# Another layout of SBUF for the weight ring, the tokens and small tensors of a two-block transformer kernel

## The reference, cut to what matters

```python
def swiglu(h, w_in, w_out):
    a, b = jnp.split(h @ w_in, 2, axis=-1)      # w_in: 1024 x 5632
    return (jax.nn.silu(a) * b) @ w_out         # w_out: 2816 x 1024

proj = h @ w_in          # each mixer: 1024 x 1048 to 1024 x 4104
out = mixed @ w_out      # each mixer: 1024 x 1024
kv = rmsnorm(s, kv_norm) @ kv_w                              # 1024 x 1536, shared KV of NSA
jax.nn.silu(flat @ cmp_w1) @ cmp_w2                          # its compress step, w2: 256 x 64
```

## Time and profile before

| what | value |
|---|---|
| median of three runs | 1311.67 us |
| lowest, highest run | 1310.64, 1311.71 us |
| span of the profiled execution (first to last instruction) | 1310.3 us |
| mean granted TensorE clock | 0.992 |
| TensorE matmul busy | 1270.2 us, 97% |
| TensorE weight loads busy (beside the matmuls) | 1077.6 us, 82% |
| VectorE, ScalarE, GpSimd busy | 873.9, 613.6, 24.2 us |
| bytes read from HBM | 216.04 MB, 166 GB/s over the span |

### The profile page before, as it was taken

How to read it: one execution, slowest core, us unless ns; L and a number is a source line. 1 busy time by engine, 2 the same in 40 slices (tenths; PEclk the granted TensorE clock), 3 DMA queues, 4 the chain that set the end, 5 groups by cost and what they waited for, 6 DMA issues and landing times.

```text
span 1310.3 us, 16491 instructions
## 1 busy us (share of the span) xinstructions
PE 1270.2 (97%) x6717; PEld 1077.6 (82%) x6717; DVE 873.9 (67%) x1312; ACT 613.6 (47%) x839; POOL 24.2 (2%) x37
## 2 busy tenths in 40 slices
PE   6999999989999999999999999999999999999997
PEld 5888888988788888878888886778888899988876
DVE  6655557885755556685657569856555567566896
ACT  6444346435434445444435357654444344544461
POOL 2000000100000000000000000000000000000000
PEclk9999999999999999999999989999999999999999
DMA  9655545443555556565665440065666686446401
GB/s 329 207 182 187 186 162 185 142 155 129 183 184 185 188 192 186 166 193 170 217 224 169 159 161 1 1 200 187 191 193 193 130 217 172 150 130 211 176 2 65
DMA packets 158812, 218.17 MB, mean 167 GB/s; under 512 B 8257, under 2 KB 110993, under 8 KB 158737
## 3 DMA queue, kind: packets, MB, share of 16 engines
q1 hardware_dynamic: 156880, 212.56, 51.2%
q0 software_dynamic: 1376, 3.71, 0.9%
q10 hardware_dynamic: 480, 0.85, 0.2%
HBM read 216.04 MB, written 1.05 MB: 166 GB/s over the span
## 4 chain that ended last, share of the span: by engine, by line
PE 82%; DVE 11%; issue 3%; ACT 2%; SPq 1%; DMA 1%; DVEq 0%
PE PS L686 23%; PE PS L689 23%; PE PS L687 23%; DVE wlo L2050 2%; PE PS L823 1%; PE PS L721 1%; PE PS L722 1%; ACT whi L1523 1%; PE PS L706 1%; PE PS L1300 1%; DVE arena L2639 1%; PE PS L728 1%; PE PS L1016 1%; SPq L591 1%; DVE XL L2090 1%
## 5 line engine op out<-in xcount | busy, mean ns | idle before, releaser
L2050 DVE TENSOR_TENSOR wlo<-raw,whi 128x2048 fp32r<-128x2048 f32 (+4 forms) x206 | 457.4, 2230 | 122.6 <-ACT whi L1523 121.8
L1523 ACT ACTIVATE whi<-raw 128x2048 fp32r<-128x2048 f32 (+4 forms) x206 | 381.4, 1863 | 63.4 <-DMA raw<-in_fox_w_in_dram 33.1
L686 PE MATMUL PS<-whi,XL 128*128 128x512 f32 (+3 forms) x992 | 385.8, 390 | 8.9 <-DVE scr L2152 3.8
L687 PE MATMUL PS<-wlo,XH 128*128 128x512 f32 (+3 forms) x992 | 379.8, 384 | 0.0
L689 PE MATMUL PS<-whi,XH 128*128 128x512 f32 (+3 forms) x992 | 265.0, 384 | 0.0
L686 PEld LDWEIGHTS PS<-whi,XL 128*128 128x128 f32 x992 | 187.3, 189 | 45.1 <-DVE scr L2152 4.9
L689 PEld LDWEIGHTS PS<-whi,XH 128*128 128x128 f32 x992 | 185.5, 190 | 35.5
L687 PEld LDWEIGHTS PS<-wlo,XH 128*128 128x128 f32 x992 | 187.4, 189 | 32.9
L1577 ACT ACTIVATE scr<-PS,rn 128x256 f32<-128x256 f32 x88 | 41.7, 474 | 225.2 <-PE PS L689 223.9
L686 PE MATMUL PS<-whi,GL 128*128 128x512 f32 x320 | 125.4, 392 | 0.0
L687 PE MATMUL PS<-wlo,GH 128*128 128x512 f32 x320 | 124.6, 389 | 0.0
(11 more groups left out here) (387 smaller groups left out, 1339.2 us busy)
## 6 DMA issues: line engine op xcount, KB each, us to landing
raw<-in_ffn_w_in_dram SPq DMA_DIRECT2D x174, 512.0 KB, 5.0
raw<-in_ffn_w_out_dram SPq DMA_DIRECT2D x88, 512.0 KB, 4.9
raw<-in_fox_w_in_dram SPq DMA_DIRECT2D x24, 512.0 KB, 7.9
raw<-in_a_w_in_dram SPq DMA_DIRECT2D x16, 512.0 KB, 4.6
raw<-in_dsa_w_in_dram SPq DMA_DIRECT2D x16, 512.0 KB, 6.0
raw<-in_kv_w_dram SPq DMA_DIRECT2D x12, 512.0 KB, 4.2
raw<-in_fox_w_in_dram SPq DMA_DIRECT2D x12, 344.0 KB, 5.0
raw<-in_a_w_out_dram SPq DMA_DIRECT2D x8, 512.0 KB, 4.9
```

The source lines that it names most:

```text
L686: mm(o, xl, wh, start=start and i == 0, stop=False, skip_group_check=True)
L687: mm(o, xh, wl, start=False, stop=False, skip_group_check=True)
L1523: A(whi[:, p % SLOTS, 0:n], raw[:, p % SLOTS, 0:n], ACT.Copy).then_inc(hi_done, 1)
L2050: V.tensor_tensor(wlo[:, p % SLOTS, 0:n], raw[:, p % SLOTS, 0:n], whi[:, p % SLOTS, 0:n].bitcast(F32), ALU.subtract).then_inc(lo_done, 1)
```

## The change

It changes addresses only.

- Each row of `whi`, `wlo` and `raw` is 2048 + 16 elements long (`SHIFT`), and the last 16 are not used, so slot s begins 64 s bytes further than it would without.
- `par`, `ss`, `rv`, `ry`, `rt`, `rr`, `nmin` and `zsum`, 1920 bytes of each partition in all, are allocated ahead of `whi` instead of behind `con`.
- `w2s`, the small weights of the compress step (1 KiB), becomes a part of `arena` (elements 12032 to 12288) instead of a tensor of its own.

The addresses that result, in bytes of a partition: `whi` 18432 (9 x 2048), `wlo` and `raw` 76224, `h` 134016, `XH` 142208, `XL` 150400, `xs` 158592, `GH` 166784, `GL` 168832, `arena` 178400. Slots of `whi` begin 64 s above a multiple of 2048, slots of `wlo` 448 + 64 s above one; the token tensors `XH`, `XL`, `GH` and `GL` begin 896 above one.

```diff
+SHIFT = 16
...
-        whi = sb("whi", [P, SLOTS, PIECE], F32R)
+        par = sb("par", [P, P])
+        ss = sb("ss", [P, 32])
+        rv = sb("rv", [P, 32])
+        ry = sb("ry", [P, 32])
+        rt = sb("rt", [P, 32])
+        rr = sb("rr", [P, 32])
+        nmin = sb("nmin", [P, 96])
+        zsum = sb("zsum", [P, 96])
+        whi = sb("whi", [P, SLOTS, PIECE + SHIFT], F32R)[:, :, 0:PIECE]
         lo_at = (nc.sbuf_base + 31) // 32 * 32
-        wlo = sb("wlo", [P, SLOTS, PIECE], F32R)
-        raw = nc.alloc_sbuf_tensor_at("raw", [P, SLOTS, PIECE], F32, offset=lo_at)
+        wlo = sb("wlo", [P, SLOTS, PIECE + SHIFT], F32R)[:, :, 0:PIECE]
+        raw = nc.alloc_sbuf_tensor_at("raw", [P, SLOTS, PIECE + SHIFT], F32, offset=lo_at)[:, :, 0:PIECE]
...
-        w2s = sb("w2s", [P, 2, 2, HD])
...
         rowsb = arena[:, 0:P]
+        w2s = arena[:, 12032:12288].rearrange("p (c k d) -> p c k d", c=2, k=2)
```

More of the change, by code:

```diff
@@ L170, in program @@
         con = sb("con", [P, C_ALL])
-        par = sb("par", [P, P])
         qgain = sb("qgain", [P, 1])
-        w2s = sb("w2s", [P, 2, 2, HD])
         bif = sb("bif", [HEADS, 3])
[L175 to L179, removed]
         lns = sb("lns", [P, 8])
@@ L184, in program @@
         r2 = sb("r2", [P, 2])
-        nmin = sb("nmin", [P, 96])
-        zsum = sb("zsum", [P, 96])
         rz = sb("rz", [P, 96])
```

## The result

The changed kernel takes 1324.84 us (median of four runs, 1322.35 to 1326.38) against 1311.66 us before; the ratio is 1.0098, with a 95% interval of 1.0081 to 1.0115. The forecast of no change was wrong. Its range, up to 1328 us, holds the time, which is that of the rival "steps of 512 columns no longer settle", 1324 us.

A forecast was written before the change was run, and what follows sets the result against it. The prediction took back-to-back weight matmuls on PE to bound the kernel, so addresses matter mainly through their spacing. Its terms summed to 0, giving 1311.5 us (no change, chance 0.37), with a range of 1297 to 1328 us.

The forecast's parts named there:

- steps of 512 columns no longer settle: Slower case for PE's weight matmuls: steps stay at their pace after a wait; 1324 us, chance 0.31.
- What bounds the kernel: Whole kernel: time is mostly the number of weight-product matmuls times the distance between them; PE holds 82% of the chain.
- terms of 0: VectorE's and ScalarE's splits (-1 to +1 us), ring loads (-0.7 to +0.7) and `w2s`: each taken as no change.
- The reading of the rows: Weight matmuls in the earlier trace: some 13 ns, 32 cycles, extra per step, taken as a cost of PE's two reads.
- PE's reading: Cost of changed operand distances within 512 bytes on PE's matmuls: taken as 0, low end -14.5 us.
- The bounds: Ends for PE's matmuls: -14.5 us, or +14 to +20 us if 3100 steps lose 4.6 to 6.6 ns, less 2.
- The slower rival: 512-column steps settle only at operand distance 0 within 512 bytes, which most slots lose; 1324 us, chance 0.31.
- sign of recognition: If distance within 512 bytes decides, pace differs by slot and products from slot 6 of `whi` stay at 226.7 ns.
- The faster rival: Weight matmuls: distance 0 makes operands collide most, so spreading slots helps; -14.5 us, 1297 us, or -3 to -8; chance 0.32.
- The rule of two independent ports: PE reads each operand through its own port, so weight loads cost no bandwidth; 512 columns every 215.7 ns, layout effect 0.
- A2: Theory added during the experiments: 512-column steps settle at 226.7 ns only with both operands at the same place within 256 bytes.

The follow-up runs named there:

- m1: Matmuls alone, model's work left out, other engines idle, 48 per segment at chosen operand distances; 512 columns take 226.7 ns at 0, 233.3 at 64 bytes.
- e2: Changed kernel without the slot spread (SHIFT 0), with a 64-byte gap ahead of `h`, so all tokens lie 64 bytes off the weights; 1332.0 us, ratio 1.0147.
- m3: Matmuls alone, 40 per segment, at further distances in 16-byte steps, for 512, 384 and 256 columns, and in bfloat16; 512 columns take 215.9 ns in bfloat16.
- e3: Changed kernel without the slot spread (SHIFT 0), with a 256-byte gap ahead of `h`; 1311.47 us, ratio 0.9998.
- e6: As e4, but FoX 344-column pieces and first mLSTM and DSA chunks are shifted too, so no FoX piece waits for one more slot; 1308.86 us, ratio 0.9966.
- e4: Changed kernel without the slot spread, except B-chunk weight pieces and a few following ones begin 64 bytes further, some loads waiting longer; 1313.09 us, ratio 1.0012.

## Why the prediction was wrong

- **What bounds the kernel** held. The whole change is in the distance from one weight matmul to the next; VectorE's splits, ScalarE's, the loads and `w2s` are where they were, as their terms of 0 said.
- **The reading of the rows** was half right. PE reads both operands from one memory and its pace at fp32r depends on where they lie: shown by m1 with nothing else at work. "It looks like a price per weight load" was wrong: the extra doesn't shrink with the block that is loaded, and it is not always 32 cycles but 16 to 51, by columns and distance.
- **The step that failed** is the choice inside the term of PE's reading: "I take 0, because the rows that differ in price (`FH`, the 344 columns) also differ by having operands off a 64-byte line, and the change keeps all of them on one." The 64-byte line does not decide it: a distance of 64 bytes, on the line, costs 6.6 ns a step (e2, m1), and one of 144, off it, settles at 226.7 (m3). What counts is the place within 256 bytes. In place of 0 the runs showed +3.9 ns on some 3870 steps of 512 columns, +15.1 us, less 1.7 in the B chunks. The trace of before could have warned of it. The prediction looked for steps of whole rows of 512 bytes; without that condition there are steps on the line at other distances. The 272-column chunk, whose group stands in the earlier trace rows, goes in steps of 1088 bytes, 17 x 64, so that all its operands are on a 64-byte line and its distances are 0, 64, 128 and 192 within 256 in turn. Fourteen of its steps take 210.28 - 208.53 = 1.75 us, 125.0 ns a step, which is 28 cycles above the columns and not 32 (start us, us, engine, line, count):

```profile
208.53 0.29 PE L721 MATMUL PS<-wlo,XH 128*128 128x272 f32 x1
...
209.28 1.16 PE L728 MATMUL PS<-whi,XL 128*128 128x272 f32 x8
210.28 0.39 PE L686 MATMUL PS<-whi,XL 128*128 128x512 f32 x1
```

  So being on the line did not fix the price. These rows do not say which way 512 columns would go; that took m1.
- **The bounds** held: the high end of +14 to +20 us, less 2 in the B chunks, gives +12 to +18, and +13.2 was measured. Its count was low and its price high, and that the product came out right is luck: four in five of 3888 steps were to lose 4.6 to 6.6 ns, and some 3870 lost 3.9 on average, since distances of 0 and 192 within 256 are among those that the change's slots bring, at 32 and 37 cycles.
- **The slower rival** had the mechanism, the place and the time (1324 us). Its condition, distance 0 within 512, is 256 by e3. Its sign of recognition, that products from slot 6 of `whi` would stay at 226.7, did not show: in the changed kernel the 359 steps from that slot have a mean of 230.3 ns. They stand between steps from `wlo` at other places, or in rows of four, and in m1 a run at distance 0 reaches 226.7 only with its sixth step; that this is the reason is argued, not shown. Its other sign, a pace that differs from slot to slot, did show: the means go from 228.8 (slot 2 of `wlo`) to 234.4 ns (slot 5 of `wlo`).
- **The faster rival** took distance 0 for the worst place. That is nearly so for 256 columns (120.0 at 0, 113.3 at 64) and the wrong way round for 512, which are four times as many. The change gained 1.7 us by it in the B chunks and lost 15.1 elsewhere.
- **The rule of two independent ports** in the Trainium skill ("TensorE: Matmul & The Clock Gate", Step-by-step: what each phase is for): its 215.7 ns for 512 columns is what m3 measured in bfloat16 (215.9, at both distances tried). At fp32r no layout came near it, and the layout mattered by up to 8 ns a step; there the measurement decides against the rule.

What stays open is the mechanism below this: what makes the pace depend on the two places, and why a run of 512 columns settles at a sum of 544 cycles at one place and wanders around 560 at another, while one of 256 columns can settle at 272. The runs give the table, not its cause. A spread of the slots by 256 bytes each, which A2 expects to be free, was not tried: it takes 3584 bytes of each partition, four times the 896 of the change, for which `w2s` already had to move.

## What to carry to other kernels

If a kernel is bound by back-to-back fp32r matmuls, the places of both operands within 256 bytes are a tuning knob, worth between 0.9966 (e6) and 1.0147 (e2) of the time here: measure the few distances in a kernel of matmuls alone, for each column count that matters, before any layout is changed, and keep one place for a whole run of steps. What is best for 512 moving columns (0) is among the worst for 256, so one layout for both is a compromise. And a gain on PE has to be taken without a new wait ahead of it: e4's later loads cost PE a wait and then its clock, more than the better pace brought.

## What was not expected of the hardware

- An fp32r matmul of 256 columns costs between 113.3 and 120.0 ns and one of 512 between 226.7 and 234.5 ns, by address alone, with a granted clock of 1.00 and no other engine at work (m1).
- The same in bfloat16 costs 109.2 and 215.9 ns, at both of the distances tried (0 and 32 bytes, m3).
- A constant offset of 64 bytes between tokens and weights (e2, +19 us) is worse than the change's mixture of all multiples of 64 (+13 us).
- In e4, PE waited for 2.4 of 5 us and was granted 0.66 of full speed in the 5 us that followed.
